# Norm junctions of a two-block transformer kernel: modulation groups moved to other places, sums of 64 columns, high halves first, and an earlier pipeline for the neighbourhood attention

## The reference, cut to what matters

```python
for layer in range(2):
    proj = rmsnorm(h, ln1_g[layer]) @ w_in[layer]
    ...                                   # three kinds of attention
    h = h + merged @ w_out[layer]
    h = h + square(relu(rmsnorm(h, ln2_g[layer]) @ w_ff1[layer])) @ w_ff2[layer]
```

```python
ml = (silu(c) @ w_mod[i] + b_mod[i]).reshape(3, 3, D)          # and the same of c_ctx
h  = gated_residual(h, ml, 0, swiglu(ada_in(h, g, ml, 0), ffn_w_in[i, 0], ffn_w_out[i, 0]), 0.5)
h  = gated_residual(h, ml, 1, mixer(ada_in(h, g, ml, 1)), 1.0) # i = 0: retention, i = 1: neighbourhood attention
h  = gated_residual(h, ml, 2, swiglu(ada_in(h, g, ml, 2), ffn_w_in[i, 1], ffn_w_out[i, 1]), 0.5)
```

## Time and profile before

| what | value |
|---|---|
| median of 3 runs | 3423.53 us (3421.09 to 3426.37) |
| the profiled execution | 3433.42 us, its span 3431.6 us |
| PE busy | 3254.8 us, 95% of the span |
| DVE, ACT, POOL busy | 1783.3, 1283.2, 1908.6 us |
| mean granted clock of TensorE | 0.956 of full speed |

### The profile page before, as it was taken

The page is one execution under the profiler, slowest core; times in us unless marked ns, Lnnn a source line. Parts: engine busy times, 40 slices in busy tenths (PEclk is TensorE's granted clock), DMA queues, the critical chain, the costliest instruction groups (busy, mean ns, idle before and its releaser), DMA issues.

```text
span 3431.6 us, 48872 instructions
## 1 busy us (share of the span) xinstructions
PE 3254.8 (95%) x18070; PEld 2730.4 (80%) x18070; DVE 1783.3 (52%) x2471; ACT 1283.2 (37%) x2147; POOL 1908.6 (56%) x1277
## 2 busy tenths in 40 slices
PE   7999989989998899999989999999999999998899
PEld 6677879976777898888868877788887888786798
DVE  5754766557557666444353445454435443335554
ACT  3444546334444454322232244232223222234443
POOL 6657587766585878687476024668837774001000
PEclk9998989999988899999999999999999999999999
DMA  5322345643223464334334212334333343332354
GB/s 182 106 89 84 125 149 192 202 140 111 93 92 129 165 201 169 122 129 137 113 123 130 69 56 92 110 122 134 129 116 110 126 136 105 111 105 71 102 182 158
DMA packets 120281, 430.38 MB, mean 125 GB/s; under 512 B 13856, under 2 KB 17184, under 8 KB 119728
## 3 DMA queue, kind: packets, MB, share of 16 engines
q1 hardware_dynamic: 93632, 335.24, 29.4%
q0 software_dynamic: 24576, 86.46, 7.6%
q10 hardware_dynamic: 1904, 6.36, 0.5%
HBM read 426.95 MB, written 8.85 MB: 127 GB/s over the span
## 4 chain that ended last, share of the span: by engine, by line
PE 60%; DVE 3%; POOL 2%; ACT 1%; issue 1%; DMA 1%; ACTq 0%; DVEq 0%; SPq 0%; POOLq 0%
PE ps L458 17%; PE ps L460 17%; PE ps L459 17%; DVE xlo L1586 1%; PE ps L541 1%; PE ps L484 1%; PE ps L543 1%; PE ps L542 1%; PE ps L900 1%; DVE tmp L1592 1%; POOL macc L392 1%; PE ps L877 1%; DMA raw<-in_panels 1%; POOL modraw L390 1%; PE ps L963 1%
## 5 line engine op out<-in xcount | busy, mean ns | idle before, releaser
L1531 DVE TENSOR_TENSOR wlo<-raw,whi 128x1024 fp32r<-128x1024 f32 x632 | 869.2, 1377 | 1018.5 <-ACT whi L987 991.4
L987 ACT ACTIVATE whi<-raw 128x1024 fp32r<-128x1024 f32 x632 | 668.0, 1058 | 1407.0 <-PE ps L460 973.1
L458 PE MATMUL ps<-xhi,whi 128*128 128x512 f32 (+2 forms) x3008 | 1039.7, 346 | 49.0 <-DVE xlo L1586 23.9
L459 PE MATMUL ps<-xlo,whi 128*128 128x512 f32 (+2 forms) x3008 | 1019.5, 339 | 0.0
L460 PE MATMUL ps<-xhi,wlo 128*128 128x512 f32 (+2 forms) x3008 | 1019.2, 339 | 0.0
L458 PEld LDWEIGHTS ps<-xhi,whi 128*128 128x128 f32 x3008 | 586.3, 195 | 127.4 <-issue 50.4
L459 PEld LDWEIGHTS ps<-xlo,whi 128*128 128x128 f32 x3008 | 586.6, 195 | 56.4 <-issue 1.9
L460 PEld LDWEIGHTS ps<-xhi,wlo 128*128 128x128 f32 x3008 | 585.5, 195 | 55.2
L390 POOL TENSOR_SCALAR modraw<-modraw,cs 128x512 f32<-128x512 f32 x288 | 543.2, 1886 | 27.6
L390 POOL TENSOR_SCALAR macc<-modraw,cs 128x512 f32<-128x512 f32 x36 | 69.2, 1922 | 854.1 <-PE ps L484 843.6
L390 POOL TENSOR_SCALAR mprod<-modraw,cs 128x512 f32<-128x512 f32 x252 | 451.2, 1790 | 19.0 <-POOL macc L392 0.2
(11 more groups left out here) (345 smaller groups left out, 4604.0 us busy)
## 6 DMA issues: line engine op xcount, KB each, us to landing
raw<-in_panels SPq DMA_DIRECT2D x632, 512.0 KB, 3.3
modraw<-in_mod POOLq DMA_DIRECT2D x144, 512.0 KB, 4.0
bias_by_column<-in_rpb POOLq DMA_DIRECT2D x16, 476.2 KB, 8.3
bia<-bias_by_column POOLq DMA_DIRECT2D x32, 96.0 KB, 2.7
rtab<-in_rtab ACTq DMA_DIRECT2D x2, 1312.0 KB, 7.7
wuq<-in_wuq ACTq DMA_DIRECT2D x2, 768.0 KB, 6.4
con<-in_con SPq DMA_DIRECT2D x1, 1345.5 KB, 12.2
h<-in_x SPq DMA_DIRECT2D x1, 1088.0 KB, 6.7
```

The costliest lines, as they stand in the source:

```text
L458: pe.matmul(out, w_hi, x_hi, start=start, stop=False)
L459: pe.matmul(out, w_hi, x_lo, start=False, stop=False)
L987: act.activation(whi[:, s * PW:(s + 1) * PW], raw[:, s * PW:(s + 1) * PW], ACT.Copy).then_inc(hi_split, 1)
L1531: dve.tensor_tensor(wlo[:, s * PW:(s + 1) * PW], raw[:, s * PW:(s + 1) * PW], whi[:, s * PW:(s + 1) * PW].bitcast(F32), ALU.subtract).then ...
```

## The change

- No modulation group stands in a junction any more (nor in the branch products of the first block); the 36 groups are spread over other places by new constants.
- The sums of the groups and of the norms have 64 columns (`SUM_W`) in place of one. All columns are equal, and one is read.
- `stats_first` comes after the last residual tile, just ahead of `stats_last`.
- The spread roots go to two banks, with a semaphore step for each 128 columns, so that the first half of a wide chunk can be scaled before the second half is spread. ACT waits for each half of a chunk too.
- `first_tiles` takes, for each chunk, the products with `xhi` of all three tiles first, and waits for `xlo` only then.
- In residual stages DVE updates `h` before it makes `wlo` of the next panel, not after.
- The logarithms of the retention's decays, a chain of 24 tiny steps on DVE that stood behind the retention's norm, are made in steps of one to five during a residual stage of the first block.
- At the start, three panels are loaded before the tables, not two, and only two are split before the norm.
- Neighbourhood attention: the scores of rounds 0 and 1 are made within the products of the values, in other banks; POOL adds the window to the bias; the low half of a pair's output is made a round later.

```diff
-MOD_UNIT, MOD_STICK, MOD_BRANCH = (6,), (0, 6), (1,)
-MOD_FF, MOD_FF2, MOD_RET = (2,), (3,), (2,)
-MOD_TILES, MOD_TILES2, MOD_TILES_R, MOD_CORE = (20,), (12, 24, 36), (11,), (1,)
+MOD_UNIT, MOD_STICK = (6,), (0, 6)
+MOD_FF, MOD_FF2, MOD_RET = (1,), (2,), (1,)
+MOD_TILES, MOD_TILES2, MOD_TILES_R, MOD_CORE = (4, 20), (4, 16, 28, 40), (4, 15), (0, 2)
+MOD_FF3 = (1, 5)
...
+            def windowed(c):
+
+                at = c % 2 * 768
+                pool.wait_ge(bias_in[c % 2 * 2], 32 * (c // 2 + 1))
+                pool.wait_ge(bias_in[c % 2 * 2 + 1], 32 * (c // 2 + 1))
+                bb = bia[:, at:at + 768].rearrange("p (r j) -> p r j", r=12)
+                pool.tensor_tensor(bb, bb, rtab[:, R_WIN:R_WIN + GW].unsqueeze(1).broadcast_to([P, 12, GW]), ALU.add).then_inc(bias_win, 1)
...
-                        last = pe.matmul(bank(b, 2 * j + s, 2 * j + s + 1), macc[:, s * 512 + j * P:s * 512 + (j + 1) * P], ones[:, 0:1], start=True, stop=True)
+                        o = (2 * j + s) * SUM_W
+                        last = pe.matmul(bank(b, o, o + SUM_W), macc[:, s * 512 + j * P:s * 512 + (j + 1) * P], ones[:, 0:SUM_W], start=True, stop=True)
...
+                def walk(k, js):
+                    xh, xl = xhi[:, k * w:k * w + T], xlo[:, k * w:k * w + T]
+                    if 0 in js:
+                        lane.take(nhi_ready)
+                    for j in js:
+                        wh, wl = pans[j]
+                        pe.matmul(bank(banks[j], 0, T), wh(k), xh, start=(k == 0), stop=False)
+                        pe.matmul(bank(banks[j], 0, T), wl(k), xh, start=False, stop=False)
+                    if 0 in js:
                         lane.take(nlo_ready)
...
+                    for j in js:
+                        last = pe.matmul(bank(banks[j], 0, T), pans[j][0](k), xl, start=False, stop=(k == NC - 1))
...
                 last.then_inc(stat_done, 1)
-                if mod:
-
-                    mod_group()
                 for i, c0 in enumerate(NORM_TILES[T]):
                     lane.take(diag_ready)
-                    last = pe.matmul(bank(5, c0, c0 + P), ones, sq[:, i * P:(i + 1) * P], start=True, stop=True)
-                last.then_inc(rs_spread, 1)
...
-                        if k == K // 2 and m == NC - 1 and norm:
-                            stats_first(norm)
...
                 if norm:
-                    stats_last(norm, mod_last)
+                    stats_first(norm)
+                    stats_last(norm)
...
                         else:
                             next_panel()
                     if inside:
                         lane.take(tile_done)
-                    b = lane.tile.slot(BANKS)
-                    update(m, b, T)
+                    if inside or m == NC - 1:
+                        update(m, lane.tile.slot(BANKS), T)
```

More of the change, by code:

```diff
@@ L1030, in root, with norm @@
                 n = len(NORM_TILES[T])
-                act.activation(sm[:, 48:48 + n], bank(6, 0, n), ACT.Sqrt, bias=eps[:, 0:1], scale=1.0 / D).then_inc(root_done, 1)
-            def norm(T, shifts=None, mod=False, then=None):
+                act.activation(sm[:, 48:48 + n], bank(6, 0, n * SUM_W).rearrange("p (n x) -> p n x", x=SUM_W)[:, :, 0], ACT.Sqrt, bias=eps[:, 0:1], scale=1.0 / D).then_inc(root_done, 1)
+            def norm(T, shifts=None, then=None, between=None):
                 root(T)
@@ L1073, in _, with first_chunks @@
             load_up(0)
-            for _ in range(AHEAD):
+            for _ in range(AHEAD - 1):
                 split()
-            act.wait_ge(tables_in, 16)
+            def first_chunks(c):
+                if c == 0:
+                    act.wait_ge(const_in, 32)
+                    act.activation(cs[:, :], par[:, P_C:P_C + 2 * NC], ACT.Silu).then_inc(silu_c, 1)
+                elif c == 3:
+                    split()
             for layer in range(DEPTH):
-                norm(T1, mod=layer > 0)
+                norm(T1, between=first_chunks if layer == 0 else None)
                 if layer == DEPTH - 1:
@@ L1341, in swiglu @@
             def swiglu(layer, j, T, norm_=None, mod=False, mod_after=()):
-                norm(T, shifts(layer, j, T), mod, then=ACT.Silu)
+                norm(T, shifts(layer, j, T), then=ACT.Silu)
                 def pair(i):
@@ L1570, in inverse_roots, with norm @@
                     dve.tensor_scalar(sq[:, i * P:(i + 1) * P], con[:, C_ID:C_ID + P], sm[:, 52 + i:53 + i], None, ALU.mult).then_inc(diag_ready, 1)
[L1571 to L1575 removed]
+            def norm(T, gains, w, shifts=None, between=None):
                 inverse_roots(T)
@@ L1635, in residual @@
                             dve.wait_ge(panel_done, lane.panel.value())
+                        elif e == ends - 1 and not inside:
+                            next_panel(lambda: update(m, lane.tile.slot(BANKS), T))
                         else:
@@ L1688, in _, with third_panel @@
                 g1 = lambda c: [(0, T1, par[:, L + P_LN1 + c:L + P_LN1 + c + 1])]
-                norm(T1, g1, T1, mod=layer > 0)
+                def third_panel(c):
+                    if c == 4:
+                        split()
+                norm(T1, g1, T1, between=third_panel if layer == 0 else None)
                 T = width1(layer)
```

250 lines of the change are left out of this document (133 added, 117 removed).

## The result

The changed kernel takes 3365.6 us (median of four runs, 3358.6 to 3373.7) where the kernel before takes 3424.9: ratio 0.9837, 95% interval 0.9818 to 0.9856. Timed again beside the experiments it took 3362.1, ratio 0.9824 (0.9800 to 0.9849). By ratio or by medians, 56 to 63 us are gone; the forecast was 42, at 3381. The profiled execution took 3370.7 us, span 3368.9.

What follows compares the result with a forecast made beforehand. PE was taken as the bound, with a chain over three engines at junctions. Gains of 83 us less 13 and 28 gave 42 off the median: 3381 us, own range 3366 to 3396, eight in ten 3350 to 3404.

Steps and rivals of the forecast that it cites:

- the term for the width: Sums in groups and norms: 64 columns cost about what one does, at most 23 us at half clock; no gain counted.
- Rival 3: The clock holds in ten junctions through 64-column sums and shorter waits: 15 to 20 us more gained, 3364 us; chance 0.15.
- The first sums' wait, 15.6 us: Eight-panel residual stages: updating ahead of the split stops DVE lagging, so three waits for accumulated squares go, 15.6 us.
- First sums behind the tile, 9 us: Nine junctions and the end: first sums run inside PE's wait for the last square, nearly 1 us each, 9 us.
- Groups out of the junctions, 21: Seven junctions: without the modulation group, and with half-chunk spreading, scaling starts sooner, 3 us each, 21 us.
- the norm's pace, 15: Norms at junctions: high halves first, and low halves at 480 ns in wide norms where POOL is idle, 15 us.
- 13 + 28: Costs: 13 us of PE work for the seven moved groups, 28 us of PE standing still for POOL, clock included.
- The stalls: PE waits for POOL's groups: about 10 and 12.5 us in the first block's `w_ff1`, 2 us twice where `MOD_FF3` follows.
- The decays, 9 us: Ahead of the retention: moving the 24 steps beside residual tiles removes a 7.08 us wait and its clock fall, 9 us.
- The attention, 12 us: Neighbourhood attention: 6.8 us a pair saves 5 to 6 us, start and last rounds 6 to 7: 12 us.
- The signs: Expected in the profile after: squares' waits under 1 us except at the start, `xlo` at 480 ns in most wide norms.
- Rivals 2 and 4 to 6: POOL keeps up (3357, 0.12); POOL late with the bias (3388 to 3397, 0.12); no net change (3422, 0.04); slower (0.04).

Runs made afterwards that it cites:

- the second profile: The changed kernel again with no edit, profiled a second time beside the experiments; timed there at 3362.1 us, 0.9824 of the kernel before.

## Why the prediction came out as it did

The direction and the range were right; the time was 15 us above the result (19 above the second timing). Point by point:

- **The clock.** This is most of the gap, as far as the runs can tell. The sum had 4 us for it, beside small parts of the junctions' terms; the runs have 68 us less at 1.2 GHz than before, up to 34 us of work. The step that failed is the term for the width: the sum weighed only what 64 columns might cost and gave them no gain, and without them the changed kernel takes 16 to 19 us more. Rival 3, with a chance of 0.15, had the time, 3364, but only part of the mechanism: it put the gain into the junctions, through wide sums and shorter waits together. There the new order alone, with sums of one column, halved the time at the lower clock (147 to 75 us); every junction still has a fall, and the width acts outside, behind the groups in the stages of small products. The row that was held against the rival, "the clock fell in junctions with only 1.67 us idle before the sums", stood behind sums of one column, so it couldn't tell the causes apart; as it turned out the clock falls there with 0.83 us idle and 64 columns too. That the width alone does nothing in the kernel before was in neither the sum nor the rival.
- **3381 twice.** That the changed kernel with narrow sums takes the forecast to the microsecond is luck. The sum had nothing for the waits in the stick attention (14 us by stage with wide sums, one of the two left with narrow ones) and 36 us for the junctions that gave 29 to 31, and the attention's stretch gave more than its 12.
- **The first sums' wait, 15.6 us.** 13.4 us went. The cause was in part right: the update's place is worth 5.7 us of waits (19.5 against 13.8 in total). It was the work of three edits together: of the 15.6 us, 2.2 are left in the changed kernel, 7.8 with the update behind the split, 4.2 with the groups back, and 4.5 with the first sums inside the tile. The groups' move took the split from 2.03 to 1.23 us. The prediction had that contention in the norms and overlooked it in the residual stages.
- **First sums behind the tile, 9 us.** The waits for the last square went from 20.3 to 10.8 us in ten places, as worked out. Undone in the changed kernel it costs 14 to 17 us, of which waits are 9.3. The price of a 64-column sum was right, 2.00 us a group against 1.95, and 3.64 against 3.55 at the lower clock, though one pair of rows it was read from mixed the clocks: the eight one-column records of 1.05 us in the earlier trace rows stand ahead of the fall, the eight of 128 columns behind it.
- **Groups out of the junctions, 21, and the norm's pace, 15, against 13 + 28.** The net was forecast at 5 us lost; 6 to 9 lost were measured, within the noise of nothing. The nine junctions gave 29 to 31 us in all (232.2 to 203.3 and 200.8), not 36, and 10 of these are there with the groups still in seven of them. Against it stand the stalls.
- **The stalls.** In `w_ff1` 11.28 and 11.06 us where 10 and 12.5 were worked out (11.23 and 5.62 in the second profile), behind `MOD_FF3` 2.23 us twice where it was 2 twice. Missed: the two of 2 us in the stick attention, whose clock made them 7 us each. The sum did not look at these two slots, where POOL had 4.5 and 0.8 us to spare before and the wide sums bring PE sooner. Moving one of them by one head was the cheapest repair of all.
- **The decays, 9 us.** No wait of 7 us is left ahead of the retention. The term was not tested by itself. By stage, from the end of the first three tiles to the last product with a panel before the retention's first sums (at 1973.7 and 1929.2 us), 202.3 us became 197.4 with one group more in it, and 193.7 with the groups back where they were: 7 to 9 us.
- **The attention, 12 us.** By itself 15 in its stretch, less 2.9 that POOL's additions to the bias cost in the norm ahead: 12. In the changed kernel the stretch is 24 us shorter; 5 of the other 9 belong to the first sums, 4 are open. The pair takes 6.2 us, not 6.8: the add takes 1.84 us where 2.1 was put, and POOL's ring of 6.44, a little longer than PE's work, hardly shows; the wait of 1.45 in every second round is gone. The loss in that norm is a step the prediction did not take: its list of norms with an idle POOL left out that the bias falls into just this one, and that its window additions were now POOL's.
- **The start, 1 us.** The first three tiles end at 35.3 and 34.3 us, where they ended at 37.7: 2 to 3 us. Not tested by itself.
- **The signs.** Two failed beside those named: one wait for accumulated squares is 1.54 us, not under 1, and a second wide norm, the one with the bias, is above 480 ns.
- **Rivals 2 and 4 to 6** did not happen: groups took as long as put, rounds are bound by PE, and POOL is late in six slots, by over 3 us in two.

## What to carry to other kernels

Where a clock can fall, price a wait by what PE does behind it: here 2 us of waiting in a stretch of small products cost 7 us, 11 us of waiting in a stretch of large ones about 14. Small sums that PE must do anyway can be made wider at next to no cost where their time hardly depends on the width (1.95 and 2.00 us here). What it gives shows only where nothing else is late: in the kernel before, PE came sooner to a slot for which POOL wasn't ready, and the gain was gone. So test such an edit on top of the others as well as alone, and when an edit makes an engine faster, check what it will now wait for. And when work is moved from one engine to keep another free, look at every place where the two now meet or part, not only at the one it was moved for.

## What the runs showed of the hardware

- The clock fell with PE never idle: in the 23 us across a group of one-column sums PE is busy throughout and granted 0.78, in the kernel before and in two others; across the same group with 64 columns it is granted 1.00.
- DVE's instruction with two inputs in SBUF: 480 ns with POOL idle, 833 beside a whole modulation group, 688 on average in the norm with two of POOL's additions of 768 columns. There all of the loss is beside the additions (3.02 and 2.07 us for two instructions, in place of 0.88), none beside POOL's issuing of transfers. The split, a `TENSOR_TENSOR` of 1024 columns, 1.23 and 2.03 us. The Trainium skill (SBUF — State Buffer, Who interferes with whom) has both cases under one rule, that such an instruction contends with GpSimd's reads of SBUF; the rows agree.
- One kernel's profiled execution can stand 0.25% off its median with another clock (before: 3433.4 us at 0.956, where the mean of 44 runs is 0.960). Differences of 10 us need the mean clock of many runs beside the trace, or the same stretch compared in several profiles.
